# Column sums of a modulation vector taken two at a time, between the matmuls of a feed-forward stage

## The reference, cut to what matters

```python
def conv_glu_ffn(h, w_up, conv_w, w_down):      # in each of the two layers; w_up: 1024 x 5632
    u = h @ w_up
    u = depthwise_conv(u, conv_w)               # 3 taps along the tokens
    gate, up = jnp.split(u, 2, axis=-1)
    return (jax.nn.silu(gate) * up) @ w_down

cond = jax.nn.silu(c)                           # second block; c: 1 x 1024
mod = cond @ ada_w[l] + ada_b[l]                # ada_w: 1024 x 6144
sh1, sc1, g1, sh2, sc2, g2 = jnp.split(mod[:, None, :], 6, axis=-1)
```

## Time and profile before

| | |
|---|---|
| median of 3 runs | 2705.35 us (2704.01 to 2706.07) |
| profiled execution | 2706.09 us, its span from the first to the last instruction 2703.9 us |
| PE busy | 2646.0 us, 98% of the span |
| DVE, ACT, POOL busy | 1823.1, 1134.5 and 353.1 us |
| granted TensorE clock, mean | 0.998 of full speed |
| chain that ended last | PE 84%, DVE 10%, ACT 3% |

### The profile page before, as it was taken

How to read it: one execution, slowest core, us unless ns; L and a number is a source line. 1 busy time by engine, 2 the same in 40 slices (tenths; PEclk the granted TensorE clock), 3 DMA queues, 4 the chain that set the end, 5 groups by cost and what they waited for, 6 DMA issues and landing times.

```text
span 2703.9 us, 55964 instructions
## 1 busy us (share of the span) xinstructions
PE 2646.0 (98%) x24551; PEld 2417.2 (89%) x24551; DVE 1823.1 (67%) x2786; ACT 1134.5 (42%) x1844; POOL 353.1 (13%) x217
## 2 busy tenths in 40 slices
PE   8999999999999999999999999999999999999998
PEld 7988998999999999988898899999987788877886
DVE  7744345556888746934335555888836998887887
ACT  6333335524333324423324624333323345466664
POOL 1211122230111000211122221111100000010001
PEclk9999999999999999999999999999999999999999
DMA  4211322364343343211232263334332322399996
GB/s 149 75 50 35 98 84 65 118 195 148 125 135 124 133 139 108 86 50 35 77 93 77 75 191 122 118 125 141 116 115 75 107 81 99 144 384 386 396 392 253
DMA packets 114203, 373.19 MB, mean 138 GB/s; under 512 B 13072, under 2 KB 14240, under 8 KB 113568
## 3 DMA queue, kind: packets, MB, share of 16 engines
q1 hardware_dynamic: 88848, 303.97, 33.2%
q10 hardware_dynamic: 18592, 41.92, 4.4%
q0 software_dynamic: 6512, 23.62, 2.4%
HBM read 336.44 MB, written 31.94 MB: 136 GB/s over the span
## 4 chain that ended last, share of the span: by engine, by line
PE 84%; DVE 10%; ACT 3%; DMA 1%; issue 1%; POOL 0%; SPq 0%; DVEq 0%; ACTq 0%; POOLq 0%
PE PS L316 83%; DMA RING<-wts 1%; DVE ARENA L1218 1%; DVE ARENA L846 1%; DVE HR L482 1%; DVE RINGR L311 1%; ACT ARENA L408 0%; PE PS L3270 0%; PE PS L1425 0%; DVE ARENA L848 0%; DVE H L492 0%; DVE ARENA L813 0%; ACT ARENA L410 0%; DVE ARENA L815 0%; DVE WR L3259 0%
## 5 line engine op out<-in xcount | busy, mean ns | idle before, releaser
L316 PE MATMUL PS<-HR,HIGHR 128*128 128x264 f32 (+1 forms) x2976 | 845.1, 284 | 0.0
L316 PEld LDWEIGHTS PS<-HR,HIGHR 128*128 128x128 f32 x2976 | 561.3, 189 | 0.8
L316 PE MATMUL PS<-XR,HIGHR 128*128 128x264 f32 (+2 forms) x1760 | 546.1, 310 | 6.0 <-ACT STAGE L612 5.3
L300 ACT CAST HIGHR<-RING 128x1024 fp32r<-128x1024 f32 (+2 forms) x340 | 330.7, 977 | 289.9 <-DMA RING<-wts 111.1
L316 PE MATMUL PS<-XR,RINGR 128*128 128x264 f32 (+1 forms) x1568 | 445.5, 284 | 0.0
L316 PE MATMUL PS<-HH,HIGHR 128*128 128x264 f32 (+2 forms) x1472 | 424.4, 288 | 2.9 <-DVE RINGR L311 1.4
L316 PE MATMUL PS<-HH,RINGR 128*128 128x264 f32 (+2 forms) x1472 | 421.4, 286 | 0.0
L311 DVE TENSOR_TENSOR RINGR<-RING,HIGHR 128x1024 fp32r<-128x1024 f32 (+2 forms) x272 | 311.3, 1149 | 118.0 <-ACT HIGHR L300 118.0
L316 PEld LDWEIGHTS PS<-XR,HIGHR 128*128 128x128 f32 x1760 | 331.8, 189 | 39.4 <-issue 19.4
L316 PE MATMUL PS<-ARENA 64*64 64x64 f32 (+10 forms) x7946 | 296.9, 240 | 12.3 <-DVE ARENA L1218 2.9
L316 PEld LDWEIGHTS PS<-XR,RINGR 128*128 128x128 f32 x1568 | 296.5, 189 | 0.0
(11 more groups left out here) (446 smaller groups left out, 5134.4 us busy)
## 6 DMA issues: line engine op xcount, KB each, us to landing
RING<-wts SPq DMA_DIRECT2D x324, 512.0 KB, 3.6
ARENA<-wmoe SPq DMA_DIRECT2D x204, 512.0 KB, 6.8
RING<-wts SPq DMA_DIRECT2D x52, 256.0 KB, 3.1
gates<-STAGE ACTq DMA_DIRECT2D x48, 264.0 KB, 4.3
ARENA<-gates ACTq DMA_DIRECT2D x48, 264.0 KB, 2.9
ys<-RING ACTq DMA_DIRECT2D x16, 512.0 KB, 7.1
RING<-wts SPq DMA_DIRECT2D x16, 384.0 KB, 3.1
ys<-STAGE POOLq DMA_DIRECT2D x8, 512.0 KB, 6.1
```

What stands on the lines that cost most here:

```text
L300: e.copy(k.highR[:, hs, 0:n], k.ring[:, i % NRING, 0:n]).then_inc(*k.s["hi"].done(i))
L316: return e.matmul(out, lhsT, rhs, start=start, stop=stop, skip_group_check=True)
```

## The change

The sums over partitions of the ada steps i - 2 and i - 1 are both taken at an even step i (2 to 48) and none at an odd one: two matmuls into two columns of one PSUM bank, with one signal to DVE behind the second. DVE writes both columns of MOD at the end of that step. Since a tile now waits up to two steps for its sum, there are three accumulation buffers (ADAB has 384 columns instead of 256), and the first multiplication of step i waits for the sums that were taken at the last even step before i.

```diff
+def ada_at(k, i):
+    return k.adab[:, 128 * (i % 3):128 * (i % 3) + 128]
+
+
+def ada_done(i):
+    return range(i - 2, i) if i and i % 2 == 0 else ()
+
+
 def ada_sum_pe(k, e, w, i):
 
     s, banks = k.s, k.banks
-    if i > 0:
-        b = banks.place(w, ("ada", i - 1))
-        w.wait_ge(*s["ada_dve"][i - 1, 7])
-        mm(e, k.PS[:, b, 0:1], k.adab[:, 128 * ((i - 1) % 2):128 * ((i - 1) % 2) + 128], k.c("one")[:, 0:1], True,
-           True).then_inc(*s["ada_pe"].done(i - 1))
+    if ada_done(i):
+        b = banks.place(w, ("ada", i))
+        for c in ada_done(i):
+            w.wait_ge(*s["ada_dve"][c, 7])
+            ins = mm(e, k.PS[:, b, c - i + 2:c - i + 3], ada_at(k, c), k.c("one")[:, 0:1], True, True)
+        ins.then_inc(*s["ada_pe"].done(i))
         banks.emptied_by(b, 1, "ada_dve", (i - 1, "mod"))
 
 
 def ada_mod_dve(k, e, w, i):
 
     s, at = k.s, k.banks.at
-    if i > 0:
-        c = i - 1
-        w.wait_ge(*s["ada_pe"][c])
+    for c in ada_done(i):
+        w.wait_ge(*s["ada_pe"][i])
+        src = k.PS[:, at["ada", i], c - i + 2:c - i + 3]
...
@@
-        acc = k.adab[:, 128 * (i % 2):128 * (i % 2) + 128]
+        acc = ada_at(k, i)
...
-        if i >= 2:
-            w.wait_ge(*s["ada_pe"][i - 2])
+        if i >= 3:
+            w.wait_ge(*s["ada_pe"][(i - 1) // 2 * 2])
@@
-    k.small, k.adab, stage = sbt("SMALL", 700), sbt("ADAB", 256), sbt("STAGE", 2 * T)
+    k.small, k.adab, stage = sbt("SMALL", 700), sbt("ADAB", 384), sbt("STAGE", 2 * T)
```

More of the change, by code:

```diff
@@ L1826, in ada_mod_dve @@
     s, at = k.s, k.banks.at
-    if i > 0:
-        c = i - 1
-        w.wait_ge(*s["ada_pe"][c])
+    for c in ada_done(i):
+        w.wait_ge(*s["ada_pe"][i])
+        src = k.PS[:, at["ada", i], c - i + 2:c - i + 3]
         if 8 <= c < 16 or 32 <= c < 40:
-            ins = e.tensor_scalar(k.MOD[:, c:c + 1], k.PS[:, at["ada", c], 0:1], k.col("ada_b_2", c), 1.0, ADD, ADD)
+            ins = e.tensor_scalar(k.MOD[:, c:c + 1], src, k.col("ada_b_2", c), 1.0, ADD, ADD)
         else:
-            ins = e.tensor_scalar(k.MOD[:, c:c + 1], k.PS[:, at["ada", c], 0:1], k.col("ada_b_2", c), None, ADD)
+            ins = e.tensor_scalar(k.MOD[:, c:c + 1], src, k.col("ada_b_2", c), None, ADD)
         ins.then_inc(*s["ada_dve"].done((c, "mod")))
```

## The result

| | before | after |
|---|---|---|
| median of 20 runs each | 2705.30 us (2700.12 to 2709.07) | 2709.41 us (2706.26 to 2713.81) |
| ratio, 95% interval | | 1.0020 (1.0014 to 1.0026) |
| profiled execution, its span | 2706.09, 2703.9 us | 2709.43, 2707.3 us |

The change makes the kernel 4.1 us slower. 2709.6 was predicted, +4.2 to the 2705.35 that was known then. (The two medians alone make 1.0015.)

A forecast was written before the change was run, and what follows sets the result against it. A two-step loop over PE and DVE was taken to bound the up steps. Layer terms of 2.16 and 2.03 us made +4.2 on 2706.09, 2710.3; less 0.74, a median of 2709.6 us, range 2704.5 to 2712.8.

The forecast's parts named there:

- A loop of two steps over PE and DVE gates the up steps: Up steps: PE waits 0.36 us every two steps in layer 0, for DVE's low part; a pair takes 24.14 us.
- The sums: On PE: a sum costs 0.225 us, two in a row 0.45, so pairing saves nothing; value 0.
- The place of the sums: Up steps: both sums fall in the gating even-step loop (layer 0), +0.225 us a pair; eight and nine pairs gated.
- The sum: Whole kernel: 2.16 us in layer 0 and 2.03 in layer 1 make +4.2 us; predicted median 2709.6 us.
- The second column hidden behind POOL: DVE's gating section: a second column of MOD could add 0.13 us to each of 17 pairs; taken as 0.
- POOL within DVE's line 2031: Gating section: POOL, starting 0.43 us after this DVE line, might be held, up to 0.11 us a pair, 1.9 us.
- Item 4: Second column of MOD in DVE's gating section: taken as 0, with bounds of +3.0 to +6.4 us for the total.
- No difference: Rival, up steps: the odd loop's slack gives DVE a lead that carries over; 2705.4 us, chance 0.17.
- The gate vanishes: Rival, up steps: POOL's collision leaves DVE's gating section and all PE waits go, 5.8 us at most; 2699.6 us, chance 0.06.
- Bank turns: Rival, later stages: they meet other PSUM banks, PE waits 0.6 to 1.2 us each; four make 2713 us, chance 0.09.
- The down steps: PE is full there and DVE has 7.43 of 16.24 us of work, so 4 pairs cost what 8 sums cost: 0.

The follow-up runs named there:

- before, column early: Kernel before, with DVE's column of MOD written in its idle time, before the taps of p = 1 instead of behind them; ratio 0.9986.
- changed, tile early: Changed kernel, with the first 3 of 8 instructions of the next ada step done in DVE's idle time, before the taps of p = 1; 2698.05 us.

## Why the prediction was right

- *A loop of two steps over PE and DVE gates the up steps.* Shown: taking 1.16 us out of DVE's section removed every wait, and what was added in the shadow of the section cost 0.1 us, what was added in the loop 3.7.
- *The sums.* 0.45 us for a pair, exactly as the series of one-column matmuls gave. Nothing is saved on PE by pairing.
- *The place of the sums.* +0.225 us for each gated pair, eight and nine pairs: right in place and number. The waits grew from 0.36 to 0.59 and from 0.31 to 0.55 us.
- *The sum.* 2.2 and 2.0 us were predicted for the layers, and the stretches show 2.5 and 1.65. In each, the last sum of the kernel before costs 0.14 us just inside the stretch and that of the changed kernel lies behind it. The first steps, left out in the prediction, and rounding are +0.1 us in each. The rest, +0.4 and -0.3 us, is in the ordinary distances of PE's matmuls, a term that the prediction did not have: on the mean (of those under 0.15 us) 121.52 ns before and 121.72 after in layer 0, 120.60 before and 120.44 after in layer 1. Most of the other kernels with pairs differ in the same way from those with a sum at every step; the one with more sums at even steps does not in layer 0 (121.58). The banks that the results go to differ between them, but that this is the cause was not tried.
- *The total.* That 4.1 us were measured where 4.2 were predicted is in part luck. The 1.0014 to 1.0026 of the runs allow for 3.8 to 7.0 us, and in the stretches errors of +0.3 us in one layer and -0.4 in the other cancel. What the stretches bear out without luck is the place, the number and the size of the waits.
- *The second column hidden behind POOL.* Right, for 0.11 of 0.13 us. What is left, 0.02 us a pair, is POOL's line, which took 1.33 instead of 1.32 us, and rounding.
- *POOL within DVE's line 2031.* Item 4 had up to 0.11 us a pair for it, in case POOL was held as in step 1. In the gating section POOL came 0.43 us behind that line's start and ran 1.33 us, as it did 0.56 us behind (1.32): it was not held. It took longer when it came 0.18 or 0.24 us behind (1.49 and 1.43 us) and ended 1.67 us after the start, as if its 1.32 us had begun 0.35 us after it (1.67 - 1.32, an estimate); DVE's row ends at 0.49. The up steps of layer 0 in the 13 profiles bear this out: POOL came 0.14 to 0.32 us behind that line 31 times and ended 1.66 to 1.68 us after its start each time; it came 0.43 or 0.44 us behind 33 times and took 1.32 to 1.34 us each time. In layer 1, with 512 elements instead of 528, it came 0.16 to 0.30 us behind 16 times and ended 1.62 to 1.63 us after the start, and it came 0.42 or 0.43 us behind 38 times and took 1.28 to 1.30 us. DVE's line took 0.48 or 0.49 us in all 118 cases.
- *The rivals.* "No difference" fell with DVE's idle time before the section, which is now 1.75 us and still thrown away at the copy. "The gate vanishes" has the right size: the kernels without waits are 5.1 to 5.8 us faster in the up steps. But it needs a shorter DVE section, as with DVE before POOL, and the change does not make that. Bank turns made no wait of PE that the profile shows.
- *The down steps* cost the same for pairs as for single sums: layer 0's are 0.1 us longer than before, layer 1's 0.14, which is the last sum that had been counted in the up steps.

## What to carry to other kernels

Where one engine waits for another a little at every second step, look for the loop: from an end on the first engine over the second one's section back to a start on the first. What work costs there depends on where it lies: 17 sums more cost 0.1 us in the shadow of that section and 3.7 us in the loop, and the change itself cost 4.1, though its total work is the same. And where the engine that is waited for sits idle within the loop, look for instructions to move into that idle time. Here 3 of 8 instructions of each step moved gave 5.5 us, and one instruction of 0.13 us in each step moved gave 5.1, since it also decided who came first at a collision.

## What the runs showed of the hardware that was not expected

- The collision of DVE's line 2025 with POOL's line 2074 is decided by a few hundredths of a microsecond. POOL coming 0.03 us after the start of line 2025 went first (1.32 us), and the two DVE instructions took 2.72 us; POOL coming 0.20 us after it took 1.75 us, and they took 2.52. In the feed-forward stages of the 13 profiles POOL's recorded start lies 0.027 to 0.047 us behind the start of such an instruction 49 times: POOL ran on every time (1.29 to 1.32 us) and DVE was held (1.86 to 1.93 us). It lies 0.051 to 0.218 us behind 205 times: DVE ran on every time (at most 0.77 us) and POOL was held (1.69 to 1.90 us). The two nearest cases, first from the timelines of DVE and POOL of the kernel before, profiled again, then from those of the kernel with three buffers:

```profile
709.11 1.93 DVE L2025 SCALAR_TENSOR_TENSOR ARENA<-ARENA,COLS 128x528 f32<-128x528 f32 x1
...
709.16 1.32 POOL L2074 TENSOR_TENSOR ARENA<-ARENA 128x528 f32<-128x528 f32 x1 [10.12 <-ACT ARENA L1931]
...
731.45 0.77 DVE L2025 SCALAR_TENSOR_TENSOR ARENA<-ARENA,COLS 128x528 f32<-128x528 f32 x1
...
731.50 1.90 POOL L2074 TENSOR_TENSOR ARENA<-ARENA 128x528 f32<-128x528 f32 x1 [10.14 <-ACT ARENA L1931]
```

- A step after a gate starts slowly: the second distance is 0.20 us instead of 0.12, whether the wait was 0.25 or 0.76 us long. These 0.08 us are part of each wait in the table.
- Outside the up steps the same kernel, profiled twice, differs by 1 to 2 us in single stretches. In some of them the granted clock is below 1 for a part. The windows of the kernel before (the third column from the end is the granted clock):

```profile
1170.00:1220.00 50.00, 46.90 (x1135) 42.12 (x1138) 18.19 (x29) 13.05 (x24) 5.57 (x3) 0.93 0.13 37
2325.00:2365.00 40.00, 36.13 (x228) 31.64 (x227) 29.88 (x75) 18.23 (x31) 2.09 (x3) 0.96 0.50 187
```

The same windows in its second profile:

```profile
1170.00:1220.00 50.00, 46.94 (x1158) 42.45 (x1158) 18.71 (x30) 13.18 (x24) 5.71 (x3) 0.93 0.12 38
2325.00:2365.00 40.00, 37.37 (x228) 32.68 (x226) 29.94 (x72) 18.27 (x28) 2.09 (x3) 0.91 0.50 185
```

  In the first window PE runs many small matmuls with gaps (busy 46.9 of 50 us in both), in the second it waits now and then for DVE and ACT (36.1 and 37.4 of 40 us). In the first the mean clock is the same, 0.93 and 0.93; in the second it differs between two executions of one program, 0.96 and 0.91. Narrower windows give 0.50 in short stretches and 1.00 between them. In the first window the first profile has two of these, 1176.2 to 1179.5 and 1213.7 to 1217.0 us, and the second one twice as long, 1175.4 to 1182.0. In the second window the first profile has one, 2333.3 to 2336.6, and the second two, 2332.5 to 2335.8 and 2339.3 to 2342.6. The clock is not all of it: between the same two matmuls, from 500.32 to 600.44 us in the first profile and from 501.40 to 600.30 in the second, lie 100.12 and 98.90 us, at a granted clock of 1.00 in both. What makes that difference is open.

- The mean granted clock of a run goes with its time. Of 67 further runs of the kernel before, the median is 2702.82 us at a mean clock of 0.998 (22 runs), 2704.60 at 0.997 (19), 2706.38 at 0.996 (19) and 2707.61 at 0.995 (5): 1.8 us for each 0.001 by a straight line through all. This is much of what the rest of the span varies by, and it hides an effect of 2 us in a single run. Two runs of other kernels do not follow the line: 2707.91 us at 0.946 (before, column early) and 2701.05 us at 0.964 (changed, tile early), within 7 us of their kernels' medians; why is open.

- It does not explain all that the two kernels with more sums cost outside the up steps. Against that line the 20 runs of the changed kernel lie 4.8 us too high on the mean, the 5 of the kernel with more sums at odd steps 8.6 and the 5 of that at even steps 10.7. The up steps account for 4.1, 4.2 and 7.9 of these, so 0.7, 4.4 and 2.8 us are left. So the extra time of these two is not the chance of the one execution that was profiled. The kernel with one more column, whose profile has as long a rest (2228.2), is another matter: that execution was the slowest of its ten, 2714.19 us against a median of 2707.93. Of the profiles' difference to the changed kernel one part can be placed. Between two matmuls that the changed kernel starts at 2305.71 and 2403.88, 98.17 us apart at a granted clock of 0.98, the odd one takes 1.9 us longer at 0.97 and the even one 3.7 longer at 0.95. What sets this off is open.
